# Another order of work in the opening norm stage of a hybrid decoder layer

## What is computed

```python
mod = silu(c) @ w_ada + b_ada                      # one row for the prompt, one for each sample
sh_m, sc_m, g_m, sh_f, sc_f, g_f = split(mod, 6)
xn = rmsnorm(x, rms_mix_g) * (1.0 + sc_m) + sh_m
q, k, v, ... = split(xn @ w_in)                    # then attention, recurrence, MLP
```

## Time and profile before

| | |
|---|---|
| median of 3 runs (range) | 2310.03 us (2308.55 to 2314.59) |
| profiled execution: own time, span | 2309.12 us, 2307.3 us |
| PE matmul busy | 2270.7 us, 98% of the span |
| DVE, ACT, POOL busy | 1438.6, 1065.7 and 845.3 us |
| granted TensorE clock, mean | 0.998 of full |

### The profile page before, as it was taken

The page is one execution under the profiler, slowest core; times in us unless marked ns, Lnnn a source line. Parts: engine busy times, 40 slices in busy tenths (PEclk is TensorE's granted clock), DMA queues, the critical chain, the costliest instruction groups (busy, mean ns, idle before and its releaser), DMA issues. The chain is left out here.

```text
span 2307.3 us, 46246 instructions
## 1 busy us (share of the span) xinstructions
PE 2270.7 (98%) x18425; PEld 2152.5 (93%) x18425; DVE 1438.6 (62%) x2595; ACT 1065.7 (46%) x2146; POOL 845.3 (37%) x1051
## 2 busy tenths in 40 slices
PE   7999999999999999999998999999999999999999
PEld 5899999989899999999887999999999999999999
DVE  5667686777777676765887334337545545554556
ACT  6666666666666666654423320135333332332331
POOL 1144352626354444535443125442323322222222
PEclk9999999999999999999999999999999999999999
DMA  7213121221312221311999322121111111111113
GB/s 299 91 50 103 41 90 56 79 71 57 102 57 94 60 93 53 103 43 49 350 343 353 126 88 78 47 62 37 46 46 47 46 46 48 54 46 46 47 47 99
DMA packets 75057, 213.20 MB, mean 92 GB/s; under 512 B 15578, under 2 KB 23642, under 8 KB 74842
## 3 DMA queue, kind: packets, MB, share of 16 engines
q1 hardware_dynamic: 73690, 206.05, 26.8%
q10 hardware_dynamic: 1152, 4.19, 0.4%
HBM read 175.49 MB, written 26.26 MB: 87 GB/s over the span
## 5 line engine op out<-in xcount | busy, mean ns | idle before, releaser
L172 PE MATMUL h_G<-xn_hi,h_w_hi 128*128 128x344 f32 x1368 | 457.3, 334 | 0.2 <-ACT h_d_oraw L918 0.2
L172 PE MATMUL h_G<-xn_hi,h_w_lo 128*128 128x344 f32 x1368 | 437.0, 319 | 0.0
L172 PE MATMUL h_G<-xn_lo,h_w_hi 128*128 128x344 f32 x1368 | 436.6, 319 | 0.0
L2462 POOL TENSOR_TENSOR h_w_lo<-h_w_raw,h_w_hi 128x1024 fp32r<-128x1024 f32 x87 | 215.5, 2477 | 488.8 <-DVE f_y L2663 204.3
L2384 PE MATMUL t_ps<-hn_hi,h_w_hi 128*128 128x344 f32 x1024 | 327.7, 320 | 0.9 <-issue 0.9
L2384 PE MATMUL t_ps<-hn_lo,h_w_hi 128*128 128x344 f32 x1024 | 327.1, 319 | 0.0
L2384 PE MATMUL t_ps<-hn_hi,h_w_lo 128*128 128x344 f32 x1024 | 327.0, 319 | 0.0
L172 PEld LDWEIGHTS h_G<-xn_hi,h_w_hi 128*128 128x128 f32 x1368 | 258.3, 189 | 32.6 <-issue 21.2
L1203 POOL TENSOR_TENSOR h_w_lo<-h_w_raw,h_w_hi 128x1024 fp32r<-128x1024 f32 x58 | 149.3, 2574 | 367.6 <-ACT h_w_hi L780 331.9
L172 PEld LDWEIGHTS h_G<-xn_lo,h_w_hi 128*128 128x128 f32 x1368 | 257.1, 188 | 4.6
L172 PEld LDWEIGHTS h_G<-xn_hi,h_w_lo 128*128 128x128 f32 x1368 | 257.0, 188 | 0.0
(11 more groups left out here) (413 smaller groups left out, 5565.5 us busy)
## 6 DMA issues: line engine op xcount, KB each, us to landing
h_w_raw<-in_w_in SPq DMA_DIRECT2D x72, 512.0 KB, 3.7
h_w_raw<-in_w_ffn SPq DMA_DIRECT2D x66, 512.0 KB, 3.6
h_d_ada_w<-in_w_ada SPq DMA_DIRECT2D x32, 512.0 KB, 4.2
g_kp<-in_cache_k SPq DMA_DIRECT2D x32, 512.0 KB, 6.9
g_vp<-in_cache_v SPq DMA_DIRECT2D x32, 512.0 KB, 5.5
h_w_raw<-in_w_mix SPq DMA_DIRECT2D x24, 512.0 KB, 3.6
x<-in_xT SPq DMA_DIRECT2D x16, 516.0 KB, 7.1
n_ada_w<-in_w_ada SPq DMA_DIRECT2D x16, 512.0 KB, 13.4
```

Of the source, the lines that this page charges most:

```text
L172: ins = eng.matmul(out, w[:, k * P:(k + 1) * P], x[:, k, columns], start=(k == 0 and n == 0), stop=(k == n_k - 1 and n == 2))
L2462: pool.tensor_tensor(wlo[buf(n)][:, :], raw[n % 2][:, :], whi[buf(n)][:, :].bitcast(F32), ALU.subtract).then_inc(w_lo.sem, 1)
```

## The change

On PE, `pieces(k)` moves ahead of `ada(k+3)` and `pick(k+2)` in each turn. On ACT, `read_ada(0)` moves in behind the second third of the reciprocal root, ahead of the last; `add_bias(0)` comes ahead of `read_ada(1)`; `read_ada(2)` and `add_bias(1)` leave the part ahead of the loop, and each turn ends with `add_bias(k+1)` and then `read_ada(k+2)` in place of `read_ada(k+3)` and `add_bias(k+2)`; `split(2)` goes from turn 4 to turn 6. On DVE, `rows(k)` is cut in `scale_rows(k)` (for row 0 in three column thirds, each as soon as its third of the reciprocal root is there) and `sample_rows(k)`, and `rest(k-1)` comes between the two.

```diff
--- before.py
+++ after.py
@@ -321,23 +321,22 @@
                 act.activation(rs[:, cols(j)], SP_[:, j, 0:TH], ACT.Ln, bias=c["eps"][:, 0:1]).then_inc(lnd.sem, 1)
                 act.wait_ge(lnd.sem, j + 1)
                 act.activation(rs[:, cols(j)], rs[:, cols(j)], ACT.Exp, scale=-0.5).then_inc(rstd.sem, 1)
+                if j == 1:
+                    read_ada(0)
             act.wait_ge(vec_in.sem, 16)
-            read_ada(0)
+            add_bias(0)
             read_ada(1)
-            add_bias(0)
-            read_ada(2)
-            add_bias(1)
             for k in range(KT):
                 act.wait_ge(normed.sem, k + 1)
                 act.activation(x[:, k, 0:T], x[:, k, 0:T], ACT.Identity, scale=c["mod"][:, scale + k, 0:1],
                                bias=c["mod"][:, shift + k, 0:1]).then_inc(scaled.sem, 1)
                 act.wait_ge(scaled.sem, k + 1)
                 act.activation(hi[:, k, :], x[:, k, :], ACT.Copy).then_inc(high.sem, 1)
-                if k + 3 < KT:
-                    read_ada(k + 3)
+                if k + 1 < KT:
+                    add_bias(k + 1)
                 if k + 2 < KT:
-                    add_bias(k + 2)
-                if k == KT // 2:
+                    read_ada(k + 2)
+                if k == KT - 2:
                     split(2)
 
         @block.tensor
@@ -394,11 +393,11 @@
             pick(1)
             pe.wait_ge(lnd.sem, NP)
             for k in range(KT):
+                pieces(k)
                 if k + 3 < KT:
                     ada(k + 3)
                 if k + 2 < KT:
                     pick(k + 2)
-                pieces(k)
 
         @block.gpsimd
         def _(pool):
@@ -456,9 +455,16 @@
             ch.sync()
             ch(dve.tensor_scalar(c["lb"][:, 1, :], c["lb"][:, 0, :], -1.0, 1.0, ALU.mult, ALU.add))
 
-            def rows(k):
-
-                ch(dve.tensor_tensor(x[:, k, :], x[:, k, :], rs[:, :], ALU.mult))
+            def scale_rows(k):
+
+                for j in range(NP if k == 0 else 1):
+                    c = cols(j) if k == 0 else slice(0, NT)
+                    if k == 0:
+                        dve.wait_ge(rstd.sem, j + 1)
+                    ch(dve.tensor_tensor(x[:, k, c], x[:, k, c], rs[:, c], ALU.mult))
+
+            def sample_rows(k):
+
                 dve.wait_ge(mod_in.sem, k + 1)
                 m, s = mod[:, scale + k, :], x[:, k, T:NT]
                 ch(dve.tensor_scalar(m, m, 1.0, vec[:, gain + k:gain + k + 1], ALU.add, ALU.mult))
@@ -471,11 +477,12 @@
                 dve.wait_ge(high.sem, k + 1)
                 dve.tensor_tensor(lo[:, k, :], x[:, k, :], hi[:, k, :].bitcast(F32), ALU.subtract).then_inc(low.sem, 1)
 
-            dve.wait_ge(rstd.sem, NP)
-            rows(0)
+            scale_rows(0)
+            sample_rows(0)
             for k in range(1, KT):
-                rows(k)
+                scale_rows(k)
                 rest(k - 1)
+                sample_rows(k)
             rest(KT - 1)
 
             dve.wait_ge(rot_in.sem, 16)
```

## The result

The changed kernel takes 2314.18 us in the median of 20 runs, the kernel before 2309.52 in 20 runs beside them. The ratio is 1.0019, 95% interval 1.0013 to 1.0025: 4.4 us more (3.0 to 5.8). The forecast was 2312 in a range of 2307 to 2316, no difference of more than 0.3%, with 2.08 us of loss. The time lies in the range, and the loss is under 0.3%, as forecast; its size was forecast at half.

The account below looks back on a forecast made before the run. PE was taken to set the norm stage's pace once row 0 starts. -1.70 + 1.48 - 1.85 + 1.14 + 1.70 + 1.31 = +2.08 us on 2310.03 gave 2312.1, called 2312, range 2307 to 2316.

Parts of the forecast that it names:

- Start of row 0: Norm stage: row 0's first product on PE at 29.74 instead of 31.44, 1.70 us earlier.
- PE's order: Norm loop: moved `ada(3)` and `pick(2)` add 1.48 us; waits add 1.14 at rows 2 and 4, 1.70 and 1.31 at rows 6 and 7.
- The split: `split(2)` moved to turn 6: takes away 1.85 us ahead of row 5 and costs nothing ahead of row 7.
- The 1.85 us of the old split: PE's wait ahead of row 5, laid to `split(2)` in that row's ACT chain; forecast to go, -1.85 us.
- Row 0's turn: From row 0's to row 1's first product on PE: 6.12 us as before, starting at a low clock.
- the late load: Stage's end: SP's held-back load lands at 70.7, ending the stage 3.6 us later, total 2315.7; chance 0.02.
- The cover holds: Rival: shorter chain behind a pick and shorter DVE round, no new waits, -2.07 us, 2308.0; chance 0.18 in part or whole.
- the start does not move: Rival: first adaLN weights land later, row 0's 1.70 us gain is lost, 2313.8; chance 0.07.
- the clock never falls: Rival: no low clock stretch in row 0, the forecast loses 1.65 us, 2310.4; chance 0.05.
- the case of a shorter chain alone: Only the chain behind a pick under 4.32 us: last rows still wait 0.85 and 1.31, +0.1, 2310.1.
- The clock stays low: Rival: new waits put the whole loop at half clock, 26 us later, 2336 us; chance 0.03.
- A single further fall: One more drop of PE's clock in the loop: costs about 1.65 us, 2313.7.

Follow-up runs that it names:

- ada_first: Changed kernel with TensorE's order of before, adaLN product and pick ahead of the row's products; ratio 1.0004 to the kernel before.
- ada_first_split4: Changed kernel with TensorE's order of before and the third weight tile's split back in turn 4; ratio 0.9994 to the kernel before.
- low_waits: Changed kernel with GpSimd's third low part held back until VectorE has done row 7's sample columns; ratio 1.0008 to the kernel before.
- ada_first_low_waits: Changed kernel with TensorE's order of before and GpSimd's third low part held until row 7's sample columns are done; ratio 0.9989 to the kernel before.
- split_turn4: Changed kernel with the third weight tile's split back in turn 4 on ScalarE; ratio 1.0007 to the kernel before.
- split_before_bias: Changed kernel with the split moved from turn 6 to turn 1, ahead of row 2's bias; ratio 1.0003 to the kernel before.
- low_halves: Changed kernel with GpSimd's third low part as two instructions of 512 columns; one run, 49.16 us from last Exp to next stage (changed kernel 46.67).
- split_alone: Kernel before with only the split moved, from turn 4 to turn 6; ratio 0.9998 to the kernel before.
- row0_whole: Changed kernel with row 0 scaled by one 1032-column instruction; one run, 46.17 us from last Exp to next stage (changed kernel 46.67).
- split_turn1: Changed kernel with the split moved from turn 6 to turn 1, behind row 2's bias; ratio 1.0012 to the kernel before.

## Why the prediction was right, and where it was half the size

- **Start of row 0.** Forecast 1.70 us earlier, at 29.74. Measured 29.66 in the changed kernel, 1.78 earlier; counted from the Exp, 1.58, of which 0.27 had gone to `read_ada(0)`, so 1.31 in all. Right within 0.4; that the place on the trace's clock came within 0.08 is luck, since the statistics ended at 24.04 and not at the 24.56 of the forecast. That the bias and not the scaling ends last was right too (25.13 and 24.60). What I did not see is that most of this start needs no new order on PE where the clock is full (ada_first: 29.75, 6.18 after the Exp; at the low clock, in ada_first_split4, it is 7.17).
- **PE's order.** Forecast +1.48 for the moved pair, +1.14 for two waits, +1.70 and +1.31 for the last rows, together 5.63. The pair low_waits and ada_first_low_waits, which differ in nothing else, gives 38.42 - 32.84 = 5.58 us from row 0 to the next stage. Right, chain and size: in the changed kernel the waits stand ahead of rows 2, 4, 6 and 7, and none ahead of row 5. A step from row 1 to 2 is 5.08 where 5.04 was worked out, and 4.49 from row 2 to 3 (4.47). The last step is right by split_turn4 (4.18, with a wait); in the pair itself it is partly luck, for low_waits has no wait ahead of row 7 but a low clock in row 6.
- **The split.** This is the step that failed: "row 7's affine step waits for DVE until 60.3 anyway: nothing". I had looked for what queues behind the split on ScalarE, GpSimd and SP, and found the load's cover. I had not asked what GpSimd's 2.4 us stop while they run. VectorE's instruction on row 7's path was held for them: 2.12 us, shown by holding GpSimd back (low_waits), by moving it into idle time (split_before_bias) and by cutting it (low_halves). The Trainium skill has the rule (SBUF — State Buffer, "Who interferes with whom"): a VectorE instruction with two inputs in SBUF, the cores' working memory, contends with a GpSimd instruction that reads SBUF; the ports that the two share are an exclusive lock, and the order of issue decides who blocks. The runs here agree: 2.29 held behind one instruction, 1.20 and 1.22 behind two halves, and GpSimd itself held by VectorE, 2.78 instead of 2.38. In the kernel before, the same 2.39 us of GpSimd lay almost wholly in VectorE's idle time (52.32 to 54.83).
- **The 1.85 us of the old split** did go in the changed kernel. The place was right and the cause partly wrong: of the wait, 0.85 us stay when only the split is moved (split_alone), and are gone with ScalarE's new order (ada_first has no wait ahead of row 5).
- **Row 0's turn.** 6.12 us forecast, 6.60 measured in the changed kernel; 5.9 to 7.1 in the other profiles with the same order. How long the low clock lasts there differs between these executions.
- **The sum.** +2.08 forecast, +4.79 in the traces: 2.12 of the difference is the held instruction, 0.48 row 0's turn, the rest of a tenth lies in small steps. That the time still lies in the stated range is partly luck: its upper end was set by the late load and a lost start, and neither came.
- **The rivals.** "The cover holds", "the start does not move" and "the clock never falls" are refuted by the trace. In the first, the case of a shorter chain alone is summed wrongly: from the same rows row 6 is ready 8.94 us after S(4) and PE after 7.81, so the wait is 1.13, not 0.85, and that case stands at +0.4. The late load did not come: it was issued at 62.80, and the next stage follows the last product after 0.90 us, as before. "The clock stays low" did not come: PE is at 1.00 from 35 to 61. A single further fall did come, at row 6, and cost nothing because row 7 was late. The rule of the Trainium skill weighed there (TensorE: Matmul & The Clock Gate, "HAM oscillation — how this bites in real kernels") is thus borne out in part: one fall behind a wait, and not one after another through the whole loop.

## What to carry to other kernels

When work is moved to another place on one engine, look at what each engine that it sets off holds up while it runs, not only at what queues behind it: here a subtraction on GpSimd, off every path, cost 2.1 us because a VectorE instruction of 8 columns with two SBUF operands stood beside it. And before dense products are moved ahead of small ones, ask what the small ones start: here each pick starts a chain of 4.9 us on two other engines, which must end before the row after next, and once the pick stood behind the products only one turn of 4.5 us was left to cover it. Undoing that edit, holding GpSimd's subtraction back and keeping the rest gave the faster kernel.

## What the runs showed of the hardware that I had not expected

- In these runs VectorE and GpSimd hold each other up by whole instructions, in both directions, also where VectorE's is of 8 columns: 0.17 us became 2.29 (changed kernel), 2.31 (ada_first), 2.30 (row0_whole) and 1.20 and 1.22 (low_halves), always to the end of GpSimd's instruction.
- It depends on the operands. In a later stage of the changed kernel two 8-column instructions follow each other beside another subtraction of GpSimd. The first has one input in PSUM, the matmul's banks, and keeps its 0.16 us; the second has both in SBUF, and is held from 0.17 to 0.75, until GpSimd ends:

```profile
1630.70 2.65 POOL L2469 TENSOR_TENSOR h_w_lo<-h_w_raw,h_w_hi 128x1024 fp32r<-128x1024 f32 x1 [8.95 <-PE t_ps L172]
...
1632.43 0.16 DVE L2560 TENSOR_TENSOR m_t<-t_ps,keep_mod 128x8 f32<-128x8 f32 x1
1632.63 0.75 DVE L2562 TENSOR_TENSOR x<-x,m_t 128x8 f32<-128x8 f32 x1
```

- PE's granted clock fell in the middle of dense products after a wait of 1.6 us (row 6 of the changed kernel, of low_waits, row0_whole, split_turn1 and split_before_bias), while low_halves kept 1.00 through row 6 after a wait of 1.62 at the same place, and the kernel before through one of 1.85. What they differ in is not settled by these runs; split_turn4, with waits of 0.74, 0.77 and 1.12 us, did not fall.
